# The last three input-projection sections of a hybrid decoder block, each computed as seven quarter products

## What is computed

```python
h = rms_norm(x, norm1_g[l]) * (1.0 + scale1) + shift1
u = h @ w_in[l]                      # (1024 x 1024) @ (1024 x 5136)
(g_q, g_k, g_v, g_r, g_lr, d_q, d_k, d_v, gate_a, gate_b) = jnp.split(u, split_idx, axis=-1)
o_a = gla_branch(g_q, g_k, g_v, g_r, g_lr, ...)
o_b = diff_branch(d_q, d_k, d_v, cos, sin, ...)      # 4 heads; scores, softmax, p0 - lam * p1, times values
merged = jax.nn.sigmoid(gate_a) * (o_a @ w_branch_a[l]) + jax.nn.sigmoid(gate_b) * (o_b @ w_branch_b[l])
x = x + gate1 * (merged @ w_out[l])
y = hier_moe(rms_norm(x, norm2_g[l]) * (1.0 + scale2) + shift2, ...)   # 32 experts, top 2
```

## Time and profile before

| | us |
|---|---|
| median of 3 runs (lowest to highest) | 1539.99 (1537.82 to 1543.0) |
| the profiled execution, its own time | 1539.34 |
| span of its records | 1537.6 |
| PE busy in the span | 1483.5 |
| DVE busy | 513.9 |
| ACT busy | 342.0 |

### The profile page before, as it was taken

The page is one execution under the profiler, slowest core; times in us unless marked ns, Lnnn a source line. Parts: engine busy times, 40 slices in busy tenths (PEclk is TensorE's granted clock), DMA queues, the critical chain, the costliest instruction groups (busy, mean ns, idle before and its releaser), DMA issues.

```text
span 1537.6 us, 20495 instructions
## 1 busy us (share of the span) xinstructions
PE 1483.5 (96%) x8071; PEld 662.7 (43%) x8071; DVE 513.9 (33%) x1100; ACT 342.0 (22%) x670; POOL 108.2 (7%) x140
## 2 busy tenths in 40 slices
PE   7799999999999999999999999999998999999996
PEld 3444455554545555444444455543332233333332
DVE  4398432323233235522223355662111111111111
ACT  3423332323334414211111112211111011111110
POOL 1000000000000000000000001001111111111111
PEclk9899999999999999999999999999999999999999
DMA  9780201010101101011130752489999999999994
GB/s 361 253 327 2 91 0 55 0 55 0 41 0 41 28 1 28 28 41 41 41 123 0 316 190 98 167 323 337 410 408 413 410 392 386 405 410 408 403 413 161
DMA packets 77840, 292.36 MB, mean 190 GB/s; under 512 B 13280, under 2 KB 38078, under 8 KB 58817
## 3 DMA queue, kind: packets, MB, share of 16 engines
q1 hardware_dynamic: 71202, 274.51, 45.4%
q0 software_dynamic: 6560, 16.77, 4.3%
HBM read 277.47 MB, written 20.09 MB: 194 GB/s over the span
## 4 chain that ended last, share of the span: by engine, by line
PE 79%; DMA 8%; SPq 5%; DVE 4%; issue 2%; ACT 2%; POOL 0%; DVEq 0%; POOLq 0%; ACTq 0%
PE PS L730 75%; DMA R<-in_expert_w 4%; DVE R L1698 2%; DMA HT<-in_expert_w 2%; SPq L358 1%; SPq L486 1%; DMA out_rows<-R 1%; PE PS L1240 1%; PE PS L885 1%; ACT R L1361 1%; SPq L481 1%; PE PS L1274 1%; SPq L366 1%; DMA R<-in_ada_w 0%; DVE R L1690 0%
## 5 line engine op out<-in xcount | busy, mean ns | idle before, releaser
L730 PE MATMUL PS<-R 128*32 128x512 f32 (+7 forms) x3966 | 759.3, 574 | 19.5 <-DMA R<-in_ada_w 9.4
L730 PEld LDWEIGHTS PS<-R 128*32 128x32 f32 (+4 forms) x3966 | 261.5, 128 | 395.0 <-issue 374.1
L730 PE MATMUL PS<-R,HT 128*128 128x512 f32 (+1 forms) x768 | 342.7, 599 | 10.9 <-DVE HT L1695 8.1
L730 PE MATMUL PS<-HT,R 128*32 128x512 f32 (+2 forms) x1200 | 299.3, 601 | 3.8 <-DMA WK<-in_expert_w 3.3
L1690 DVE TENSOR_TENSOR R<-R,PS 128x512 f32<-128x512 f32 (+1 forms) x95 | 71.6, 772 | 449.2 <-PE PS L730 449.2
L730 PEld LDWEIGHTS PS<-R,HT 128*128 128x128 f32 x768 | 142.7, 191 | 173.8 <-issue 159.4
L1361 ACT ACTIVATE R<-PS 128x512 f32<-128x512 f32 (+4 forms) x131 | 78.4, 609 | 411.6 <-PE PS L730 273.9
L730 PEld LDWEIGHTS PS<-HT,R 128*32 128x32 f32 (+1 forms) x1200 | 101.8, 132 | 137.7 <-issue 136.7
L730 PE MATMUL PS<-WK,R 128*32 128x512 f32 (+1 forms) x496 | 109.2, 599 | 2.3 <-DMA HT<-in_expert_w 2.2
L694 POOL DMA_INDIRECT out_rows<-R x36 | 52.3, 1454 | 297.2 <-DVE R L1698 160.1
L1698 DVE SCALAR_TENSOR_TENSOR R<-PS,R,gate 128x1024 f32<-128x1024 f32 (+1 forms) x23 | 28.5, 1238 | 129.4 <-PE PS L730 129.4
(11 more groups left out here) (253 smaller groups left out, 811.6 us busy)
## 6 DMA issues: line engine op xcount, KB each, us to landing
R<-in_expert_w SPq DMA_DIRECT2D x42, 2048.0 KB, 24.4
R<-in_expert_w SPq DMA_DIRECT2D x48, 1024.0 KB, 21.1
HT<-in_expert_w SPq DMA_DIRECT2D x11, 2048.0 KB, 21.3
HT<-in_expert_w SPq DMA_DIRECT2D x18, 1024.0 KB, 11.5
R<-in_ada_w SPq DMA_DIRECT2D x16, 1024.0 KB
WK<-in_expert_w SPq DMA_DIRECT2D x7, 2048.0 KB, 24.9
R<-in_w_in SPq DMA_DIRECT2D x5, 2048.0 KB, 8.1
R<-in_ada_w SPq DMA_DIRECT2D x16, 512.0 KB
```

Of the source, the lines that this page charges most:

```text
L730: return nc.tensor.matmul(o, l, r, start=a, stop=z)
```

## The change

Sections 3, 4 and 5 (in heads 1, 2 and 3) are no longer 8 tiles over the full depth. Tokens, depth and columns are halved, and the product of 2 x 2 quarters is made from seven quarter products (512 tokens x 512 depth x 256 columns) in place of eight, with sums of quarters before and after. A quarter product is two units; a unit is two token tiles x 4 depth blocks = 8 matmuls of 256 columns, into one bank, alternately 7 and 5, later 7 alone. So a head has 14 units, numbered 0 to 13. Sums of tokens (`tok2`, `tok1s`, `tok34`), of weights (in place, in the ring) and of results are all DVE instructions. ACT copies only units 0 to 3.

```diff
+        tok = [[hT[:, 4 * k:4 * k + 4, 512 * t:512 * t + 512] for t in range(2)] for k in range(2)]
+        tok2, tok1s = (R3[:, 2048 * i:2048 * (i + 1)].rearrange("p (k t) -> p k t", k=4) for i in range(2))
+        tok34 = gate[:, :, :].rearrange("p g n -> p (g n)").rearrange("p (u k t) -> p u k t", u=4, k=4)
+        quart = [wring[:, 1, 4 * (x % 2):4 * (x % 2) + 4, 256 * (x // 2):256 * (x // 2) + 256] for x in range(4)]
+        sect = [U[:, 1], U[:, 0], R2[:, 4096:8192].rearrange("p (t n) -> p t n", t=NT)]
...
-            load_section(4, O_GR)
-            load_section(5, O_GV)
+            for n, off in ((0, O_GR), (1, O_GV)):
+                units_done(n, 8)
+                e.wait_ge(s["w_sums"], 4 * n + 4)
+                load_quarter(0, off)
+                units_done(n, 10)
+                load_quarter(2, off)
+                units_done(n, 13)
+                load_quarter(3, off)
+                units_done(n, 14)
+                load_quarter(1, off)
...
+            def product_of_pairs(b, x, q, rows):
+                for u in (2 * q, 2 * q + 1):
+                    for k in range(4):
+                        last = mm(bank(b)[:, 256 * (u % 2):256 * (u % 2) + 256], rows(u, k), quart[x][:, k, :],
+                                  k == 0, k == 3)
+                last.then_inc(s["proj_mm"], 1)
...
+            def m3(n, q):
+                e.wait_ge(s["w_sums"], 4 * n + 4)
+                added_by_vector(n, 10 if q == 0 else 13)
+                product_of_pairs(7, 1, q, tokens(1, 4))
...
+            def attend(h):
+                n = h - 1
+                scores(h, 0)
+                m1(n, 0)
+                m1(n, 1)
+                scores(h, 1)
+                m4(n, 0)
+                turn(h, 0)
+                m4(n, 1)
...
+                scores(h, 6)
+                m3(n, 0)
+                turn(h, 5)
+                weigh(h, 4)
+                scores(h, 7)
+                m5(n, 1)
+                turn(h, 6)
+                weigh(h, 5)
+                m3(n, 1)
+                turn(h, 7)
+                weigh(h, 6)
+                weigh(h, 7)
...
+            def product_read(n, j, b, dst, scale=1.0):
+                e.wait_ge(s["proj_mm"], 3 * NT + 14 * n + j + 1)
+                act(dst, bank(b).rearrange("p (x n) -> p x n", x=2), ACT.Copy, scale=scale).then_inc(s["proj_free"], 1)
...
+            def product_add(n, j, b, dst, other):
+                product_done(n, j)
+                tt(dst, other, bank(b).rearrange("p (x n) -> p x n", x=2), ALU.add).then_inc(s["prod_added"], 1)
...
+                product_done(n, 3)
...
+                tt(w22, w21, w22, ALU.add).then_inc(s["w_sums"], 1)
+                row_max(h, 2)
+                combine(h, 1)
+                e.wait_ge(s["w_sums"], 4 * n + 1)
+                tt(w21, w11, w21, ALU.subtract).then_inc(s["w_sums"], 1)
+                e.wait_ge(s["w_sums"], 4 * n + 2)
+                tt(w11, w22, w11, ALU.subtract).then_inc(s["w_sums"], 1)
+                for q in range(2):
+                    product_add(n, 4 + q, 7 - 2 * q, up_left[q], up_right[q])
+                finish(h, 0)
+                e.wait_ge(s["w_sums"], 4 * n + 3)
+                tt(w12, w12, w11, ALU.subtract).then_inc(s["w_sums"], 1)
...
+                row_max(h, 6)
+                combine(h, 5)
+                product_add(n, 11, 7, up_right[0], up_right[0])
+                finish(h, 4)
+                row_max(h, 7)
+                combine(h, 6)
+                product_add(n, 12, 7, low_left[1], low_left[1])
+                product_add(n, 12, 7, up_right[1], up_right[1])
+                finish(h, 5)
+                combine(h, 7)
+                product_add(n, 13, 7, up_right[1], up_right[1])
+                finish(h, 6)
```

More of the change, by code:

```diff
@@ L603, in stage_head @@
             def stage_head(h):
-                wait_apart(e, (s["scores_ready"], h * NT + 1))
+                e.wait_ge(s["scores_ready"], h * NT + 1)
                 e.tensor_copy(qs, qT[:, h, :])
                 e.tensor_copy(ks, kT[:, h, :]).then_inc(s["head_staged"], 1)
-            with e.Fori(1, NH) as h:
+            for h in range(1, NH):
                 stage_head(h)
@@ new lines, in turn @@
+            def turn(h, i):
+                e.wait_ge(s["att_a"], h * NT + i + 3)
+                e.wait_ge(s["aT_done"], h * NT + i + 1)
+                if h > 0 and i == 4:
+                    e.wait_ge(s["prod_added"], 14 * (h - 1) + 7)
+                for j in range(i + 1):
+                    last = nc.tensor.transpose(bank(4 + j // 4)[:, (j % 4) * P:(j % 4 + 1) * P],
+                                               attn[i % 2][:, j * P:(j + 1) * P], ident[:, :])
+                last.then_inc(s["att_tr"], 1)
@@ new lines, in weigh, with read_by_scalar @@
+            def weigh(h, i):
+                e.wait_ge(s["aT_done"], h * NT + i + 2)
+                e.wait_ge(s["att_o_done"], h * NT + i + 2)
+                if h == 0:
+                    e.wait_ge(s["proj_free"], 4 + 2 * NT + 1 + i)
+                for j in range(i + 1):
+                    last = mm(bank(6)[:, 0:DV], attnT[i % 2][:, j * P:(j + 1) * P],
+                              U[:, 2, j, h * DV:(h + 1) * DV], j == 0, j == i)
+                last.then_inc(s["att_o"], 1)
+            def read_by_scalar(n, j):
+                e.wait_ge(s["proj_free"], 4 + 3 * NT + 4 * n + j)
@@ L922, in _ @@
             e.wait_ge(s["kT_done"], NT)
-            attend(0, 2, 4 + 2 * NT + 1)
-            with e.Fori(1, NH) as h:
-                attend(h, h + 2)
+            attend_values()
+            for h in range(1, NH):
+                attend(h)
             for u in range(2):
@@ new lines, in _, with product_done @@
+            row_max(0, 0)
+            for i in range(NT):
+                if i + 1 < NT:
+                    row_max(0, i + 1)
+                combine(0, i)
+                if i >= 1:
+                    finish(0, i - 1)
+                if i < 6:
+                    first_sum(i)
+            finish(0, NT - 1)
+            def product_done(n, j):
+                e.wait_ge(s["proj_mm"], 3 * NT + 14 * n + j + 1)
+            def product_add(n, j, b, dst, other):
+                product_done(n, j)
+                tt(dst, other, bank(b).rearrange("p (x n) -> p x n", x=2), ALU.add).then_inc(s["prod_added"], 1)
```

350 lines of the change are left out of this document (229 added, 121 removed).

## The result

| | before | after |
|---|---|---|
| median, us (lowest to highest, runs) | 1538.9 (1536.84 to 1543.0, 4) | 1524.15 (1521.39 to 1524.93, 4) |
| the profiled execution: own time, span | 1539.34, 1537.6 | 1523.91, 1522.2 |

The ratio is 0.9897, with a 95% interval of 0.9883 to 0.9911. The gain is 14.75 us by the medians and 15.4 by the spans. The time forecast was 1526.3, a gain of 13.6. When it was made, the median of before stood at 1539.99 over three runs; with a fourth it is 1538.9. So the time was missed by 2.15 us, the gain by 1.15 by the medians and by 1.8 by the spans, each time in the same direction: more came off than I had said.

What follows compares the result with a forecast made beforehand. PE was taken as the bound. Per head 6.4 + 0.15 - 0.02 - 0.42 - 0.81 - 0.76 = 4.55 us, three heads 13.6, giving 1525.7 for the profiled execution and a median of 1526.3 us; range for 8 in 10: 1519 to 1536.

Steps and rivals of the forecast that it cites:

- PE as the bound: Heads 1 to 3: PE is busy without gaps, so work removed there comes off the time unless DVE or ACT delays it.
- The section matmuls: Each head: 112 matmuls of 256 columns at 0.438 us replace 64 at 0.865; 49.0 for 55.4 us, 6.4 less.
- The weight loads: 48 added matmuls a head bring no visible load cost; rival at 0.06: 0.218 us each, 31.4 us in all, 1557.7 us.
- The waits: Each head: PE waits 0.02, 0.42 and 0.81 us before turn(4), turn(5), turn(6), and 0.76 before weigh(7).
- The wait that goes: Before the cut last tile of each head, PE's wait for ACT's copy of bank 7 disappears: -0.15 us a head.
- DVE: In each head, 20.5 us of new sums make DVE busy 44.5 of some 74.5 us, hidden in its waits: nothing.
- The first rival: Chance 0.12: DVE's queue becomes the bound inside the heads, 3.0 us of waits a head beyond the forecast, some 1537 us.
- `turn(2)` as what is late next: In a head, if the cover for row_max(3) failed, turn(2) would be late next, then block 3's exponentials; costed at nothing.
- Loads, ACT, tail: Quarter and gate-weight loads hidden, 4 fewer ACT copies no gain, tail moves up whole; rival of a lost tail: 0.04, about 1540.
- The signs: Changed profile: heads 74.3 to 74.7 us, units 3.50, idle 0.3 to 0.8 before turn(5), turn(6), weigh(7), clock 1.00, DVE about 45.
- about 2 us: In the first rival: PE waits past this length would lower the granted clock and feed on themselves; longest forecast wait 0.81 us.

Runs made afterwards that it cites:

- the version with all edits: Kernel after with combine(5) and combine(6) ahead of row_max, last unit cut 6+2, unit 0 of head 1 in head 0's idle time; 1517.11 us, again 1516.67 us.
- the order on DVE: Kernel after with combine(5) and combine(6) put ahead of the next block's row_max on DVE; 1519.22 us, ratio to before 0.9873.
- the doubled load: Kernel after with a spare DVE reduction ahead of each of 12 PSUM-reading sums and 4 weight sums a head; 1526.88 us, ratio 0.992.
- the cut unit: Kernel after with unit 13 cut, 2 of 8 matmuls between weigh(6) and weigh(7), finish(6) ahead of its sum; 1520.43 us, ratio to before 0.9872.
- the narrower matmuls: Kernel before with heads written out and, in heads 1 to 3, each 512-column section matmul split into two of 256; 1540.22 us, ratio 1.0005.
- the written-out loops: Kernel before with the loops over the heads written out on all four engines, nothing else; 1539.8 us, ratio 0.9998.
- the spare matmuls alone: Kernel after with 8 unused matmuls of 128 columns ahead of turn(7) in head 0's idle time; 1525.54 us, ratio 0.9915.

## Why the prediction was right, step by step

**PE as the bound.** Right. What PE no longer does in a head came off the time, and the version with all edits shows heads in which PE is busy throughout.

**The section matmuls.** Forecast: 49.0 us a head in place of 55.4. The version with all edits, where nothing waits, lets the new ones be added up from start to start. Its 14 units take 7.06 + 3.51 + 3.54 + 6.97 + 6.97 + 6.96 + 3 x 3.51 + 2.59 + 0.86 = 49.0 us in head 2 (pairs together, the last in its two parts), 0.437 us a matmul against 0.438. In after itself the step of a pair of units, 284.07 - 277.11 = 6.96 us, gives 0.435:

```profile
277.11 7.12 PE L753 MATMUL PS<-R 128*128 128x256 f32 x32
284.07 0.49 PE L909 MATMUL PS<-ident,R 128*128 128x128 f32 x3
```

The old ones were 55.6 and not 55.4. In head 2 of before tile 0, which stands in two halves, took 7.06 us (330.52 to 334.10 and 334.86 to 338.34), tile 1 took 6.98 and the cut one 6.97 (397.74 to 402.99 and 405.43 to 407.15), where I had put 6.92 for all. So this term is 6.6 and was put at 6.4.

**The weight loads.** Here a row and a rule had disagreed. The price of 0.437 us and the 0.005 us for each added load say that the row was right. The Trainium skill ("TensorE: Matmul & The Clock Gate", Back-to-back issue gap) gives about 81 ns for load and matmul at 128 columns. By that rule I had estimated about 11 us more in a head, and the heads became 5.1 us shorter. The measurement decides: no such cost shows in this stream of 32-bit matmuls.

**The waits.** Forecast 0.02, 0.42, 0.81 and 0.76 us, together 2.01. Measured 0.00, 0.42, 0.82 and 0.76, together 2.00, and the version without them is 2.00 shorter a head. These are places and sizes worked out from the trace of before alone, by laying DVE's unchanged chain beside a shorter unit, and the experiments show that the cause was the named one: the first two go when only the order on DVE is changed, the third when two matmuls are put in front of `weigh(7)`. The terms as printed add up to 4.54 us and not 4.55, which changes nothing.

**The wait that goes.** This is the term that was mis-sized: "-0.15 a head". I took the idle time in the bracket, which leaves out the drain, though for `weigh(7)` I had added the 0.16 of the drain to the bracket. More rows of PE in head 2 of before give the steps around it:

```profile
338.34 0.27 PE L885 MATMUL PS<-ident,R 128*128 128x128 f32 x1
338.55 0.92 PE L730 MATMUL PS<-R 64*128 64x384 f32 x4
339.39 0.29 PE L730 MATMUL PS<-causal_neg,identb 128*128 128x128 bf16 x2
339.65 7.13 PE L730 MATMUL PS<-R,HT 128*128 x16
346.63 0.38 PE L885 MATMUL PS<-ident,R 128*128 128x128 f32 x2
...
396.08 1.50 PE L730 MATMUL PS<-R,WK 128*128 x12
```

From `weigh(5)` to the cut tile at 397.74 it was 1.66 us, where after the same step is 1.34 (317.27 - 315.93): 0.32 lost, not 0.15. Ahead of tile 1 the mask steps by 0.26 where 0.13 is usual: 0.13 more, without any bracket. The transpose of `turn(0)` stepped by 0.21 to what follows it, and steps by 0.11 in the version with all edits: 0.10. Together 0.55 in place of 0.15. Only the 0.32 is a wait that the trace names; it is there with the loops written out as well. With the loops written out the step of that mask falls to 0.17 (338.64 to 338.81 in head 2 of that run), so 0.09 of the 0.13 came off by the form of the loop; the step of the transpose stays at 0.20 there (337.59 to 337.79), so its 0.10 goes with the matmuls that follow it, a unit now and `scores(2)` before.

Put together for head 2: 6.62 + 0.55 - 2.00 = 5.17 us, which is 79.05 - 73.89 to 0.01. The forecast was 4.55. The 0.6 us of difference are the 0.4 by which this term was too small and the 0.2 of the old tiles. Both went the same way; no two errors had to cancel for the forecast to come near.

**DVE.** Forecast 20.5 us more in a head; it is 21.4, 18.0 and 16.9. Fourteen token sums of 1.22 us stand in the three heads, 7, 4 and 3, besides four weight sums in each: the four at the start of head 1 are not the only ones, since `tok34` is made anew inside each head. So there are 11, 8 and 7 sums of 1024 elements where the sum of 20.5 us had 8. And the sums with a PSUM operand were dearer in the forecast (0.775, over the whole span) than here. Their group in heads 1 to 3 of after:

```profile
L1828 DVE TENSOR_TENSOR R<-R,PS 128x512 f32<-128x512 f32 x36 | 24.1, 684 | 22.7 <-PE PS L753 22.7
```

Costed at nothing, and rightly: no new sum is in the list of PE's waits, and only the doubled load put one there. The first rival, DVE's queue as the bound, is thus out. (By its own terms, 9 us of waits beyond the forecast, it gives 1535.3 us and not 1537.) But I had named `turn(2)` as what is late next, and the doubled load showed bank 7 ahead of unit 6 and of unit 13 instead.

**Loads, ACT, tail.** Costed at nothing, and no unit waits for a load. (Counted from 0, as the units are, the gate weights wait for units 7 and 13.) The tail kept its length to 1.1 us, so the gain of the heads arrived at the end whole.

**The signs.** A unit stepped by 3.51 us for 3.50; the waits stand where they were named, DVE releases each, and nothing waits elsewhere; the granted clock in the heads is 1.00. Three signs were off: the heads last 73.88 us and not 74.3 to 74.7, by the 0.6 above; the bracket ahead of `turn(5)` is 0.20 and not 0.3 or more, though from start to start it is 0.36; and DVE is busy for 45.4, 42.0 and 40.9 us, not 45 in each.

## What to carry to other kernels

When a block of filler work on the bound engine gets shorter, lay the untouched chain of the other engine beside it, from start to start: the new waits can be read off the old trace, here to 0.02 us. Take a vanished wait the same way, from start to start, since the idle time in a row leaves out the drain. Where an engine works in order, what another engine waits for goes first: `combine` ahead of `row_max` gave 1.23 us a head for no work at all. Where two pieces of the bound engine are tied by a hand-over, a little independent work between them covers it: two matmuls between `weigh(6)` and `weigh(7)` gave 0.77 us a head. And one whole unit moved into a gap elsewhere gave some 2.5 us once, about what the cut unit gives in three heads.

## What the runs showed of the hardware

A 32-bit matmul with fresh 128 x 128 weights costs by its columns: 0.865 us at 512, 0.437 at 256, 0.224 at 128. 64 more of them in a head, each with its own weight load, for the same columns in all (weight loads busy for 65.28 us in place of 40.95), cost 0.3 us of 79.

At the end of head 0 PE stands idle for 2.29 us (2.58 before) in eight profiles. In six of them, those of before, of after twice, of the narrower matmuls, of the cut unit and of the doubled load, the 8 transposes behind it step by 1.5 to 1.8 us; the granted clock of the 4.2 us behind the gap is 0.59 to 0.65 in all six (0.65 in before), between full and the half that 1.2 GHz is. In the other two, the written-out loops and the order on DVE, they step by 0.93 behind the same 2.29 us, at 1.00. In all four where the gap was filled to 0.5 us or less they ran at 1.00 too, and so did the heads of after, behind waits of up to 0.60 us. That points to the idle time as a condition of the fall, though not the only one; these are twelve profiles, one for each run. None of the gaps read here lies between 0.60 and 2.29 us, so the "about 2 us" from which the prediction lets a wait feed on itself is not shown. In the profiles the fall costs 1.6 us (10.54 against 8.90 from `weigh(5)` to head 1). Since the spare matmuls alone brought no gain in the runs, what it costs over many executions stays open.
